# The token transform of a Fourier mixing as three float32r products

## The reference

```python
def fourier_mix(f):
    B, N, _ = f.shape
    fg = f.reshape(B, N, N_FOURIER_GROUPS, FOURIER_GROUP_W).astype(jnp.float32)
    y = jnp.fft.fft2(fg, axes=(1, 3), norm="ortho").real
    return y.reshape(B, N, FOURIER_W).astype(f.dtype)
...
    y = g_f * (f_mix @ w_fourier) + g_a * (att @ w_mla_o)
```

## Time and profile before

| what | value |
|---|---|
| median of 3 runs | 1646.37 us (1645.01 to 1646.57) |
| the profiled execution's own time | 1644.74 us |
| its span in the profile | 1642.9 us |
| busy share of the span, PE / DVE / ACT | 97% / 76% / 55% |
| granted clock of TensorE, mean | 0.994 |

### The profile page before, as it was taken

The page is one execution under the profiler, slowest core; times in us unless marked ns, Lnnn a source line. Parts: engine busy times, 40 slices in busy tenths (PEclk is TensorE's granted clock), DMA queues, the critical chain, the costliest instruction groups (busy, mean ns, idle before and its releaser), DMA issues.

```text
span 1642.9 us, 20508 instructions
## 1 busy us (share of the span) xinstructions
PE 1598.6 (97%) x8394; PEld 1319.0 (80%) x8394; DVE 1251.3 (76%) x1438; ACT 904.9 (55%) x1060; POOL 269.6 (16%) x185
## 2 busy tenths in 40 slices
PE   6999999999999999999999999999999999999994
PEld 4768867668989999899887778888888888888883
DVE  3535876886678656575799975699999999999994
ACT  3423245543444444352533244688888888878874
POOL 0000030000057242300000102211221221221201
PEclk9999999999999999999999999999999999999997
DMA  9216812004122414131222102699999999999993
GB/s 394 78 46 251 299 57 77 1 18 162 53 103 78 153 53 148 58 128 52 103 77 78 52 27 84 226 418 381 382 368 387 379 354 370 376 374 362 383 363 119
DMA packets 55461, 323.32 MB, mean 197 GB/s; under 512 B 12753, under 2 KB 13777, under 8 KB 18755
## 3 DMA queue, kind: packets, MB, share of 16 engines
q1 hardware_dynamic: 43584, 307.91, 49.2%
q0 software_dynamic: 9504, 8.43, 2.3%
q10 hardware_dynamic: 2274, 5.62, 0.9%
HBM read 323.99 MB, written 23.07 MB: 211 GB/s over the span
## 4 chain that ended last, share of the span: by engine, by line
PE 93%; DVE 3%; DMA 2%; ACT 1%; issue 1%; POOL 0%; SPq 0%; ACTq 0%; POOLq 0%; DVEq 0%
PE ps L590 25%; PE ps L1483 21%; PE ps L1510 11%; PE ps L1099 7%; PE ps L779 5%; PE ps L1355 3%; PE ps L1022 3%; PE ps L755 2%; PE ps L1467 2%; PE ps L812 1%; PE ps L1492 1%; PE ps L886 1%; DMA cst<-in_cst 1%; PE ps L1010 1%; PE ps L1011 1%
## 5 line engine op out<-in xcount | busy, mean ns | idle before, releaser
L2230 DVE TENSOR_TENSOR wlo<-raw,whi 128x2048 fp32r<-128x2048 f32 x248 | 565.5, 2302 | 117.6 <-ACT whi L1562 117.6
L1562 ACT ACTIVATE whi<-raw 128x2048 fp32r<-128x2048 f32 x248 | 470.4, 1912 | 143.8 <-PE ps L1483 35.2
L1483 PE MATMUL ps<-whi,xH 128*128 128x512 f32 x512 | 202.7, 396 | 0.3 <-DVE xL L2332 0.3
L1483 PE MATMUL ps<-whi,xL 128*128 128x512 f32 x512 | 200.2, 391 | 0.0
L1483 PE MATMUL ps<-wlo,xH 128*128 128x512 f32 x512 | 199.3, 389 | 0.0
L590 PE MATMUL ps<-hH,whi 128*128 128x512 f32 x352 | 138.7, 394 | 0.3 <-ACT dmax L2039 0.3
L590 PE MATMUL ps<-hH,wlo 128*128 128x512 f32 x352 | 137.1, 390 | 0.0
L590 PE MATMUL ps<-hL,whi 128*128 128x512 f32 x352 | 137.0, 389 | 0.0
L3280 POOL DMA_INDIRECT sum_scratch<-yb,idt x30 | 48.7, 1625 | 421.3 <-ACT yb L2171 421.3
L1483 PEld LDWEIGHTS ps<-whi,xL 128*128 128x128 f32 x512 | 96.1, 188 | 20.7
L1483 PEld LDWEIGHTS ps<-whi,xH 128*128 128x128 f32 x512 | 96.2, 188 | 19.5 <-DVE xL L2332 0.5
(11 more groups left out here) (522 smaller groups left out, 3514.6 us busy)
## 6 DMA issues: line engine op xcount, KB each, us to landing
raw<-in_experts SPq DMA_DIRECT2D x192, 1024.0 KB, 7.9
raw<-in_streamed SPq DMA_DIRECT2D x92, 1024.0 KB, 4.8
xT<-in_x SPq DMA_DIRECT2D x1, 2048.0 KB, 8.8
sum_scratch<-xN ACTq DMA_DIRECT2D x2, 1024.0 KB, 8.9
Y<-sum_scratch SPq DMA_DIRECT2D x4, 512.0 KB, 5.2
out<-Y SPq DMA_DIRECT2D x4, 512.0 KB, 3.0
h_scratch<-hN SPq DMA_DIRECT2D x4, 384.0 KB, 2.6
ctxT<-in_ctx SPq DMA_DIRECT2D x1, 1024.0 KB, 26.2
```

The lines of the kernel that those rows point to most:

```text
L1483: ins = e.matmul(b.t[:, :], l, w, start=(kk == 0 and i == 0), stop=(kk == 7 and i == 2))
L1562: e.activation(u.hi, u.raw, ACT.Copy).then_inc(*p.inc("hi", n, on="hi"))
L2230: e.tensor_tensor(u.lo, u.raw, u.hi.bitcast(F32), ALU.subtract).then_inc(*p.inc("lo", n, on="lo"))
```

## The change

The unit `dft` is split like the others, and the transformed columns are split too: ACT writes the high half `ABH` from the bank, DVE the low half `ABL`. Each float32 matmul of the token products becomes three float32r matmuls. `ABL` lies where `fT` lay.

```diff
-    whole = unsplit + order["dft"] + [n for j in range(4) for n in order["mod", j]]
+    whole = unsplit + [n for j in range(4) for n in order["mod", j]]
...
-    fT, AB = at("fT", PH + 2048, [4, 512]), at("AB", PH + 4096, [4, 2, 256])
+    fT = at("fT", PH + 2048, [4, 512])
+    ABH, ABL = at("ABH", PH + 4096, [4, 2, 256], FR), at("ABL", PH + 2048, [4, 2, 256], FR)
...
-        p.wait_ge(*done("dma", "u", n))
+        u = units[n]
+        p.wait_ge(*done("dve", "lo", n))
         for g in range(4):
...
+            prs = []
             for i in range(2):
                 for cs in range(2):
-                    ins = e.matmul(b.t[:, :], AB[:, g, i, cs * 128:(cs + 1) * 128],
-                                   units[n].raw[:, i, cs * 512:(cs + 1) * 512], start=(i == 0 and cs == 0),
-                                   stop=(i == 1 and cs == 1))
-            ins.then_inc(*p.inc("fb", g))
+                    l, r = slice(cs * 128, (cs + 1) * 128), slice(cs * 512, (cs + 1) * 512)
+                    prs += tri((ABH[:, g, i, l], ABL[:, g, i, l]), (u.hi[:, i, r], u.lo[:, i, r]))
+            mm(e, b.t[:, :], prs, p.inc("fb", g))
...
         fourier(3)
+        convert(U_DFT[0])
+
+        def fourier_high(g):
+            p.wait_ge(*done("pe", "ab", g))
+            copy(ABH[:, g, :, :], ps["ab", g].t[:, :].rearrange("p (i c) -> p i c", i=2), p.inc("abh", g))
+
+        fourier_high(0)
         root(3)
...
         def fourier_columns(g):
-            p.wait_ge(*done("pe", "ab", g))
-            copy(AB[:, g, :, :], ps["ab", g].t[:, :].rearrange("p (i c) -> p i c", i=2), p.inc("ab", g))
+            p.wait_ge(*done("act", "abh", g))
+            TT(ABL[:, g, :, :], ps["ab", g].t[:, :].rearrange("p (i c) -> p i c", i=2), ABH[:, g, :, :].bitcast(F32),
+               ALU.subtract, "ab", g)
...
         fold(3)
+        convert(U_DFT[0])
         fourier_columns(0)
```

More of the change, by code:

```diff
@@ L1684, in act_program @@
         square(4, 0, kvraw[:, 512:768], "pe", "sum", 3, 0)
+        fourier_high(1)
         root(4)
@@ L1689, in act_program @@
         ahead = 2
+        for g in (2, 3):
+            fourier_high(g)
         for n in U_DFT:
```

## The result

| what | before | changed |
|---|---|---|
| median of 15 runs | 1645.08 us (1643.92 to 1647.22) | 1649.58 us (1646.98 to 1651.78) |
| ratio, 95% interval | | 1.0023 (1.0016 to 1.0029) |
| profiled execution, span | 1642.9 us | 1647.4 us |
| mean granted clock, profiled execution | 0.994 | 0.991 |

What follows compares the result with a forecast made beforehand. The prediction took PE, busy 97% of the span, to bound the kernel. Its terms, -3.00 for the products and +3.02 for the stall, summed to 0.0 us, so 1646.4 us on the median, range 1643.6 to 1649.6 us.

Steps and rivals of the forecast that it cites:

- its own sign of being wrong: Listed observations that would refute the prediction, among them a granted clock below 1.00 between 98 and 110 us.
- the first rival: PE's silence before the third normalisation's spread lowers its clock: 0.9 to 5.5 us, middle 3.2, so 1649.6 us; chance 0.10.
- yardstick of 3.3 us: Whole kernel: some 0.2% that a measurement can tell from no change; more than this counts as slower, chance 0.10.
- Products: Token transform: sixteen float32 matmuls, 13.93 us, become 48 float32r matmuls, 10.93 us as in neighbouring L779; saves 3.00 us.
- Stall: Spread of the third normalisation: PE waits 3.24 us for DVE's `rst` instead of 0.22, costing 3.02 us.
- forward count: Table conversion on ACT and DVE timed instruction by instruction from the old rows, bringing `rst` to an end at 101.54, before 98.52.
- Cover: Next weight units' conversions, ready about 113.8 us, wanted by PE at 117.1: 3.3 us left, so no wait.
- The clock: At the 3.24 us gap before the spread: unbroken 2.4 GHz expected, since the program's end fell after 3.7 us; fall given 0.10.
- The low end of that price: Clock fall costs 0.9 us, from the program's first sixteen L638 records taking 1.94 us against a later 1.07.
- the high end: Clock stays down over all light products from 98.58 to 103.18, 4.6 us doubled, plus the start's 0.9: 5.5 us.
- The sum: Whole kernel: -3.00 us from token matmuls plus 3.02 us of waiting gives 0.0; no change, chance 0.80.

Runs made afterwards that it cites:

- the late load: Changed kernel with SP's load of the first gate unit held back until the token products are done, as before the change; 1650.09 us, ratio 1.0027 to before.
- only ACT's `convert` early: Changed kernel with ACT's high-half table conversion moved ahead of the last group's copy, DVE's low half left behind the fold; 1647.54 us, ratio 1.0008 to before.
- the gap alone: Kernel before, float32 products kept, with two unread subtractions added on DVE behind the last fold; 1652.70 us, ratio 1.0048 to before.
- the filled gap: Changed kernel with twelve dummy float32 matmuls on PE in front of the spread that waits for DVE; 1646.29 us, ratio 1.0004 to before.

## Why the prediction was right or wrong

The time lies in the range, but the account of the prediction does not hold: its sum has the clock unbroken, and its own sign of being wrong, a clock below 1.00 between 98 and 110 us, came true. That the time is in the range is in part luck. The upper end was the middle of the first rival, whose price came out too small, and the kernel before measured 1645.08 us this time and not 1646.37: the same distance of 4.5 us from the older median would have been outside. By its own yardstick of 3.3 us the result is slower, a case that it gave 0.10.

- **Products:** -3.00 forecast, -2.83 measured. Nearly all of the 48 records run at the spacing of the neighbour; of the 0.17 us that are missing, 0.11 lie between the first and the second, which start 0.34 us apart, and they do so in the runs with the clock at 1.00 too. There PE goes over from float32 to float32r; that this is the reason no run tests.
- **Stall:** 3.02 forecast, 2.97 measured. Each step of the forward count holds when the 0.56 us are taken off by which the stage began later: the high half at 95.11 (forecast 94.56), the low half at 97.04 (96.50), `rst` to the end at 102.06 (101.54). The engine order decided it, as said.
- **Cover:** no wait of the w_fourier products; they follow the token products at 121.62 without a gap. The loads that moved are worth nothing, as the late load shows.
- **The clock: here it failed.** The step is the sentence "The new gap, 3.24 us, is a little shorter, and that speaks for an unbroken 2.4 GHz". It took the 3.7 us between the last matmul and the fall at the end of the program for the silence that is needed. In the profile of the changed kernel the fall comes 1.1 us after PE's last work, and a silence of 2.1 us has it too. The case was in the list, with 0.10 where it should have had most of the chance. Its price was taken at 3.2 us, and the profile has 3.79. The low end of that price took the slow first products of the program as time at the lower level; the row of the kernel before for 14 to 16 us has the granted clock at 1.00, so no row shows that. What the high end took, all the small products slowed, is what happened, at 1.8 times their length (8.39 for 4.60) and not quite twice.
- **The sum:** +0.0 forecast. The profile has -2.83 + 2.97 + 3.79 = +3.93, the ratio says 1.0023 of 1645.1, or +3.8, and the medians +4.5.

The Trainium skill (TensorE: Matmul & The Clock Gate, section "Why this matters for your kernels") warns of idle gaps between bursts of matmuls as what throws the engine back. The runs agree: here the gap that mattered was one of 3.2 us in a kernel whose PE is busy for 97% of the span, and one of 2.1 us did the same.

## What to carry to other kernels

A wait of two or three microseconds that PE has not had before can cost more than its length, as it did in four kernels here: price the small products behind it at half speed, and give that case most of the chance, unless traces of more than one execution show a silence of that length with the clock at 1.00 behind it. Dummy matmuls in the gap bring the clock back but not the stall; moving the new work on the other engines into idle time ahead of the stage brings back both. An instruction added on an engine that looks idle (DVE at 76%) has to be followed to the next one on that engine that PE waits for.

## What the runs showed of the hardware

The fall is not tied to the silence in a fixed way. In the changed kernel the clock fell 1.1 us into the silence, in the kernel with only ACT's `convert` early 1.3 us into it (PE's last work ends at 100.45, the fall is at 101.7). In the gap alone and with the late load it fell only after PE had started again: the spread started at 101.44 and 103.61, and the stretches that have the fall in them, with a mean of 0.59 and 0.54, begin at 102.40 and 104.60, while the microsecond ahead of them is at 1.00. In the first two the load of the gate unit lands in the silence, in the other two nothing does; whether it has a part in the moment of the fall no run separates. The low level held for some 10 us of the stage in the changed kernel and for some 7 in the other three. The times of the changed kernel lie 4.8 us apart (1646.98 to 1651.78), those of before in the same measurement 3.3; that the moment of the fall makes the difference is not shown.

Nor is a silence of microseconds always needed. At the program's start, in code that is the same in all nine profiles, PE waits 0.5 us between two groups of small products. In three of the nine (the filled gap, the late load and only ACT's `convert` early) the granted clock is 0.50 soon after it, in the filled gap from 26 to 29 us, and the spread there takes 2.06 us and not 1.10 as in the changed kernel:

```profile
25.39 0.71 PE L648 MATMUL ps<-cst,rowbuf 128*128 128x2 f32 x4 [0.50 <-ACT rowbuf L1577]
25.96 2.06 PE L680 MATMUL ps<-rst,one 128*128 128x512 f32 x2
```

In the other six it stays at 1.00 there. The Fourier stage starts at 96.1 to 96.3 us in these three and at 94.0 to 95.6 in the six, so this is part of the scatter between executions. So 1.7 us of silence without a fall, in one profile and eleven times, is no promise for other places. What sets the moment of the fall these runs don't tell.
